# Moving the sum of squares of one norm from TensorE to GpSimd, and two products in pieces between the sums of the next

## The reference

```
mix = token_mixer(a, ...)                      # ends in  concat(h_ml, h_mla) @ w_out
x = x + rmsnorm_2(mix, norm_post_mix)          # "post_mix": mean of mix^2 over the channels
m = rmsnorm_2(x, norm_pre_mlp)                 # "mlp":      mean of x^2 over the channels
y = square(relu(m @ w_up)) @ w_down            # 4096 hidden channels
x = x + rmsnorm_2(y, norm_post_mlp)
```

## Time and profile before

| | |
|---|---|
| median of 3 runs | 2695.09 us (2694.74 to 2695.11) |
| the profiled execution | 2693.12 us |
| its span, first to last instruction | 2691.4 us |
| mean granted TensorE clock | 0.994 |
| PE busy | 2595.1 us (96%) |
| DVE busy | 1857.9 us (69%) |
| ACT busy | 1042.9 us (39%) |
| POOL busy | 1224.1 us (45%) |

### The profile page before, as it was taken

One profiled execution on the slowest core, in us unless ns is written; L12 is line 12 of the kernel. 1 busy time (PEld: TensorE's weight loads), 2 busy tenths in 40 slices (PEclk: granted clock), 3 DMA queues, 4 the chain that ended last, 5 costly groups with the idle time before them and its releaser, 6 DMA issues.

```text
span 2691.4 us, 32407 instructions
## 1 busy us (share of the span) xinstructions
PE 2595.1 (96%) x12366; PEld 2089.7 (78%) x12366; DVE 1857.9 (69%) x2108; ACT 1042.9 (39%) x1447; POOL 1224.1 (45%) x763
## 2 busy tenths in 40 slices
PE   7999999999999999999998999989998999999998
PEld 5888787887777888887886788656885888877777
DVE  7565665457658666668879647766558666778887
ACT  5223343323124333234435111756555433434444
POOL 2222222233447888884333433241135888723331
PEclk9999999999999999999999999999999999999999
DMA  5333333244332433245641343401323554754543
GB/s 192 118 102 114 121 94 126 83 152 155 130 130 63 118 102 111 81 133 199 215 137 55 132 152 101 126 1 46 131 83 84 172 155 147 220 156 160 164 141 141
DMA packets 335840, 339.49 MB, mean 126 GB/s; under 512 B 19723, under 2 KB 254838, under 8 KB 335686
## 3 DMA queue, kind: packets, MB, share of 16 engines
q1 hardware_dynamic: 329446, 313.81, 37.3%
q10 hardware_dynamic: 6240, 23.59, 2.3%
HBM read 228.55 MB, written 107.77 MB: 125 GB/s over the span
## 4 chain that ended last, share of the span: by engine, by line
PE 52%; DVE 10%; issue 2%; ACT 1%; DMA 1%; POOL 1%; SPq 0%; DVEq 0%; ACTq 0%; POOLq 0%
PE ps L3712 36%; PE ps L566 9%; DVE op_lo L3789 2%; PE ps L2784 2%; PE ps L2807 1%; DVE sw_lo L3622 1%; PE ps L2794 1%; DVE acc L4033 1%; DVE acc L4040 1%; PE ps L3288 1%; DVE acc L2310 0%; DVE x L2731 0%; DMA x_block<-acc 0%; DVE op_lo L3692 0%; PE ps L3673 0%
## 5 line engine op out<-in xcount | busy, mean ns | idle before, releaser
L3712 PE MATMUL ps<-op_hi,sw_hi 128*128 128x512 f32 x1769 | 693.2, 392 | 15.8 <-DVE op_lo L3789 8.4
L3712 PE MATMUL ps<-op_hi,sw_lo 128*128 128x512 f32 x1769 | 689.7, 390 | 0.0
L3712 PE MATMUL ps<-op_lo,sw_hi 128*128 128x512 f32 x1769 | 689.5, 390 | 0.0
L3712 PEld LDWEIGHTS ps<-op_hi,sw_hi 128*128 128x128 f32 x1769 | 332.8, 188 | 96.6 <-issue 16.7
L3712 PEld LDWEIGHTS ps<-op_hi,sw_lo 128*128 128x128 f32 x1769 | 332.8, 188 | 69.7
L3712 PEld LDWEIGHTS ps<-op_lo,sw_hi 128*128 128x128 f32 x1769 | 333.0, 188 | 68.9 <-issue 0.5
L532 POOL TENSOR_TENSOR w_hi_t<-w_raw,ones 128x1024 fp32r<-128x1024 f32 (+1 forms) x60 | 118.5, 1978 | 531.1 <-DMA w_raw<-in_w_in 238.0
L3612 ACT ACTIVATE sw_hi<-sw_sumNone 128x512 fp32r<-128x512 f32 (+1 forms) x252 | 157.1, 624 | 332.2 <-PE ps L3712 250.0
L3622 POOL TENSOR_TENSOR sw_lo<-sw_sumNone,sw_hi 128x512 fp32r<-128x512 f32 x138 | 213.8, 1559 | 34.2 <-ACT sw_hi L3612 34.1
L3573 POOL TENSOR_TENSOR sw_sumNone<-sw_raw 128x512 f32<-128x512 f32 (+1 forms) x63 | 113.8, 1806 | 232.1 <-DVE sw_lo L3622 209.3
L3612 ACT ACTIVATE sw_hi<-sw_raw 128x512 fp32r<-128x512 f32 (+1 forms) x189 | 117.5, 622 | 198.1 <-PE ps L3712 196.4
(11 more groups left out here) (500 smaller groups left out, 5423.5 us busy)
## 6 DMA issues: line engine op xcount, KB each, us to landing
op_raw<-hidden SPq DMA_DIRECT2D x42, 1024.0 KB, 8.7
w_raw<-in_w_in SPq DMA_DIRECT2D x47, 512.0 KB, 4.6
sw_raw<-in_w_ffn_in SPq DMA_DIRECT2D x44, 512.0 KB, 5.2
hidden<-hidden_blocks SPq DMA_DIRECT2D x13, 1536.0 KB, 6.1
hidden<-hidden_blocks SPq DMA_DIRECT2D x14, 1280.0 KB, 5.0
sw_raw<-in_w_up SPq DMA_DIRECT2D x32, 512.0 KB, 8.6
sw_raw<-in_w_down SPq DMA_DIRECT2D x32, 512.0 KB, 5.5
acc<-proj SPq DMA_DIRECT2D x30, 512.0 KB, 4.5
```

The costliest lines, as they stand in the source:

```text
L3712: mm = pe.matmul(out, w, x[:, k, :], start=(k == 0 and i == 0 and r < 4), stop=(k == n - 1 and i == 2), skip_group_check=r >= 4)
```

## The change

*First half.* The eight sums over partitions on PE (32 small matmuls) go. The ring of two buffers becomes an accumulator and one buffer: ACT writes the squares of tile 0 to `sq_first0` and those of tiles 1 to 7 to `sq_first1`; POOL adds the second to the first after each tile (`first_squares`, seven instructions). PE sums the accumulator once over the partitions (`first_square_sum`, 4 matmuls), ahead of `half_spread(1)`. ACT's square of tile n (n from 2) now waits for POOL's add of tile n-1. ACT's copy of product M2 (`first_act`) also waits for PE's one sum. POOL's first three adds stand in front of the low part of the last unit's weights, the other four behind it and in front of all that POOL does for the MLP.

*Second half.* The two fp32 products M2+2 and M2+3 are cut in four pieces (`product_block`) of one instruction each, and one piece of each is issued behind every second tile of the loop.

```
             def behind(i):
-                for n in {3: (0, 1), 4: (2, 3, 4), 5: (5, 6, 7)}.get(i, ()):
-                    square_sum3(pe, 0, n)
                 for n in {4: (0, 1), 5: (2, 3)}.get(i, ()):
                     x3_turn(pe, 0, n)
...
             x3_turn(pe, 0, 5)
+            first_square_sum(pe)
             half_spread(pe, 1)
...
+        def first_squares(pool, n):
+            pool.wait_ge(*count("x3_squared", n + 1))
+            if n > 1:
+                pool.wait_ge(*count("x3_summed", n - 1))
+            a, b = sq_ring[0]
+            pool.tensor_tensor(a[:, :], a[:, :], b[:, :], ALU.add).then_inc(count("x3_summed", 0)[0], 1)
+
+        def first_square_sum(pe):
+            pe.wait_ge(S["rstd_ready"], NORM_AT[PM[0]] + 1)
+            pe.wait_ge(*count("x3_summed", KT - 1))
+            for c in range(4):
+                mm = pe.matmul(PS[2][:, c * P:(c + 1) * P], sq_ring[0][0][:, c * P:(c + 1) * P], ones[:, :],
+                               start=(c == 0), stop=True, skip_group_check=True)
+            mm.then_inc(count("x3_summed", 0)[0], 1)
...
-                act.activation(sq_ring[t][n % 2][:, :], acc[:, XO[t][n], HT[t]], ACT.Square)\
+                act.activation(sq_ring[t][n % 2 if t else min(n, 1)][:, :], acc[:, XO[t][n], HT[t]], ACT.Square)\
...
+        def product_block(pe, m, k):
+            p, r = SEQ[m]
+            if k == 0:
+                pe.wait_ge(*count("sw_sum", 4 * p + {1: 2, 6: 4}[r]))
+            if r == 6:
+                pe.wait_ge(*count2("b_hi", KT + k + 1))
+            else:
+                pe.wait_ge(*count2("t_made", 2 * k + 2))
+            mm = pe.matmul(bank(p, r), weight_block(p, r)[:, k * P:(k + 1) * P], fresh_of(p, r)[:, k, :],
+                           start=(k == 0), stop=(k == 3))
+            if k == 3:
+                mm.then_inc(S["s_product"], 1)
...
             act.wait_ge(*count("s_product", done(p, 0)))
...
+            if p == P2:
+                act.wait_ge(*count("x3_summed", KT))
...
             for n in range(KT):
                 square_sum3(pe, 1, n)
                 x3_turn(pe, 1, n)
-            product_fp32(pe, M2 + 2)
+                if n % 2:
+                    product_block(pe, M2 + 2, n // 2)
+                    product_block(pe, M2 + 3, n // 2)
             norm_spread(pe, "mlp")
-            for m in range(M2 + 3, M2 + 7):
+            for m in range(M2 + 4, M2 + 7):
...
-            for n in range(2, len(TILES2)):
+            for n in range(2, len(TILES2) - 1):
                 split_lo(pool, Step(U_WO2 + n))
+            for n in (1, 2, 3):
+                first_squares(pool, n)
+            split_lo(pool, Step(U_END - 1))
+            for n in range(4, KT):
+                first_squares(pool, n)
             x3_pool(pool)
```

## The result

The changed kernel takes 2703.95 us (median of 8 runs, 2702.91 to 2705.9) against 2694.80 before (8 runs): ratio 1.0036, 95% interval 1.0027 to 1.0045. That is 9.2 us slower; 2702.7 had been forecast. The profiled execution took 2705.83 us, its span 2704.1, with a mean granted clock of 0.989.

A forecast was written before the change was run, and what follows sets the result against it. PE, 96% busy, was taken as the bound, with the spread of half 1 and PE's time from loop to M2+6 deciding. Terms 8.8 + 1.6 - 4.3 + 1.5 = +7.6 us gave 2702.7 us (+0.28%), range 2696 to 2708.

The forecast's parts named there:

- Unit 13: Matmul unit awaiting POOL's low part of its weights: starts at 2007.2, 0.2 us earlier, after PE waits 4 us.
- The half's sum of squares complete at 2026.8: DVE's last nine instructions of half 0, slowed by 7 POOL turns of 1.0 us; complete at 2016.05 before.
- The clock, +1.6: Half sums after PE's 13 us idle run at half rate: +1.6 us, bounds 0 and 3.2.
- The spread at 2030.4: Start of half 1's spread on PE, against 2021.56 before: +8.8 us, PE saving included.
- The loop, -4.3: Loop of half 1: pieces fill PE's waits, four rounds take 17.6 to 18.4 us against 22.0 with two products.
- Behind the loop, +1.5: From the loop to M2+6: extra delay from DVE's queue and perhaps the clock, bounds 0 and +3.
- the forecast's first reason: Behind the loop, DVE's own queue holds post_u2; PE's wait before M2+6 grows from 1.88 to about 3.3 us.
- The second reason: Behind the longer wait before M2+6 the clock may be at the lower level again.
- Rival 1: At block_lo DVE goes first, losing 1 to 3 turns, not 7: -1 to +2, 2694 to 2697; chance 0.13.
- Rival 2: POOL's adds find only DVE's gaps, sum of squares by about 2019: 2691, or 2689; chance 0.08.
- Rival 4: The loop's pieces hold up the next round's squares: -1 and not -4.3, 2706; chance 0.04.
- rival 3: POOL contends with DVE through pair P2+1, clock falls twice in full: +11 to +14, 2706 to 2709; chance 0.12.

The follow-up runs named there:

- after: The changed kernel with both halves of the change, against the kernel before it: 2703.95 us, ratio 1.0036.
- second execution of after: The whole change, unaltered, executed and profiled once more: 2703.29 us (one run).
- block sums: Second half of the change alone, plus DVE's last four block sums of half 1 moved ahead of its mean of norm "mlp": 2690.67 us, 0.9987 of before.
- squares only: First half of the change alone, loop and M2+2 as before, against the kernel before: 2706.32 us, ratio 1.0043.
- sum ahead: Whole change, with DVE's last add of the half's squares behind two block_lo, the half's mean behind four: 2696.57 us, 2.2 above before.
- weight sums late: Whole change, with POOL's three weight sums of the first pair moved behind two low parts and DVE's first residual of half 1: 2699.96 us.
- pieces only: Second half of the change alone, the pieces of M2+2 and M2+3 put into the kernel before: 2692.16 us, ratio 0.9989.
- PE kept busy: Whole change, with 46 small matmuls ahead of the half sum to fill PE's idle time: 2701.95 us, 2.0 below the whole change.

## Why the prediction was right, point by point

- *Unit 13* (forecast: waits 4 us, starts 0.2 earlier). It waited 4.53 us and started, corrected, at 2007.90: 0.5 later. Right that the PE time saved in front of it is all waited away. The 0.7 us between the two starts are the 0.77 that ACT's square of tile 3 waited for POOL's second add: I had ACT's split at 2003.4, it was at 2004.1.
- *The half's sum of squares complete at 2026.8.* It was at 2029.90 less 2.42, 2027.5. The seven turns of 1.0 us in DVE's last nine instructions were there: 11.45 + 1.74 against 5.38 + 0.68 is 7.1 us, and three of them measured apart are 3.07. The 0.7 us too much are those of the point above: `block_lo` started at 2014.4 where I had 2013.7.
- *The clock, +1.6.* This term was mis-sized. It rested on one row, 3.2 us of work at half rate behind 6.50 us of idle time. Here it was 5.4 us behind 10.92, and 4.5 us behind the 4.53 before unit 13. Keeping PE busy measured the term at 2.6 us.
- *The spread at 2030.4 and 1.6 more for the clock: 2032.0.* It was 2033.8: 0.7 of the difference is the sum's, 1.1 the clock's.
- *The loop, -4.3.* Measured -4.5 in after, -4.4 alone. Rounds 4.38 us, no wait.
- *Behind the loop, +1.5.* Measured +1.7 up to the late row: M2+4 stands 7.7 us late, the late row 9.4. 1.4 of it is made as the forecast's first reason had it, of PE's waits for DVE (2.22, 0.52, 1.48 and 0.33 us against 1.88, 0.94 and 0.36). The second reason, a second fall of the clock, did not happen in after; where it happened it cost next to nothing at the late row. I had a wait of 3.3 before M2+6, it was 2.22; M2+6 stands at 2072.0, where I had 2071.
- *The sum.* +7.6 was forecast, the late row has +9.4 and the median +9.2. The clock accounts for 1.1 of the 1.8 us, the sum of squares for 0.7, the term behind the loop for 0.2, and the loop gave 0.2 back. To their ends the two profiles of after show +10.3 and +10.2, 1 us of it behind the late row, which no term of the forecast has; that the median lies as near to the late row as it does is in part luck.

Rival 1 (DVE gets through) needed lengths of 0.7 in `block_lo`. Rival 2 needed the sum by 2019. Both are out by the DVE rows. Rival 4 (the loop doesn't give) is out by the rounds of 4.38 us without a wait. Of rival 3 a part came true: the clock was out in the open for longer than I had taken.

One wait remains. Behind the late row PE waits for DVE a second time, 1.33 us in before and 2.35 in after, since DVE's first instruction of a product starts late there. The profile puts DVE's idle time down to `issue`, so to nothing that it knows of. The timeline of DVE in before and in after:

```profile
2364.73 0.69 DVE L3728 TENSOR_TENSOR s_u<-ps,s_p 128x512 f32<-128x512 f32 x1 [0.48 <-issue]
```

```profile
2377.60 0.69 DVE L3760 TENSOR_TENSOR s_u<-ps,s_p 128x512 f32<-128x512 f32 x1 [1.51 <-issue]
```

The instruction reads `s_p`, and that is written by ACT. The timeline of ACT in before and in after:

```profile
2361.73 1.92 ACT L3782 ACTIVATE op_hi<-op_raw 128x2048 fp32r<-128x2048 f32 x1 [2.90 <-DMA op_raw<-hidden]
...
2364.07 0.58 ACT L3721 ACTIVATE s_p<-ps 128x512 f32<-128x512 f32 x1
```

```profile
2374.60 1.91 ACT L3814 ACTIVATE op_hi<-op_raw 128x2048 fp32r<-128x2048 f32 x1 [3.93 <-DMA op_raw<-hidden]
...
2376.94 0.58 ACT L3753 ACTIVATE s_p<-ps 128x512 f32<-128x512 f32 x1
```

ACT's copy ends 0.08 us before DVE starts, here as in all the other profiles to within 0.01 us, and it stands in ACT's queue behind a split that waits for a transfer of `hidden`. Against the late row that split starts 1.03 us later in after (1.64 us ahead of it, 2.67 in before), and DVE's instruction 1.03 us later too. So DVE waits for a transfer, by way of ACT. DVE's idle time was 1.01 us in the second execution of after, 0.17 to 0.51 in the four kernels without the squares on POOL, 0.86 to 1.51 in all with them. Why the transfer lands later with them was not tested.

## What to carry to other kernels

An instruction that is moved to an engine which shares a port with a busy one costs the busy one a whole turn, here 1.0 us, and what counts is how many turns lie in front of the result for which the bottleneck waits: here 6.5 us of work taken off TensorE cost 12 us, and changing two places in DVE's queue gave 7 of them back. Small independent products between two waits are the safe half of such a change; judge each half by itself. And before a wait is removed, look whether the next wait behind it is for the same engine: then much of what is won ends there, and so does what the clock takes: half of what I had expected of the block sums, and nearly all of the 1.7 us of M2+6 at half rate.

## What the runs showed of the hardware

- Two full queues on DVE and POOL alternate one by one, at 1.02 us of DVE per POOL instruction of 128x512 fp32. The pattern held over eight instructions in a row in before (first MLP, DVE's starts 1.70 us apart from 832.87 to 844.76, of which the earlier trace rows has two) and over five in after (from 2020.98).
- The granted clock fell to 0.50 behind waits of TensorE as short as 1.87 us (squares only) and 1.93 us (sum ahead), and stayed at 1.00 behind 1.88 (before), 2.21 (weight sums late) and 2.22 and 2.21 us (after, twice), while it fell behind 2.21, 2.21 and 2.22 us in three others (pieces only, PE kept busy, sum ahead). Of waits of this length one cannot say from their length alone whether the clock falls. In the wait of 10.92 us it fell during the wait (0.67 in the mean of 2021 to 2023 us); behind the 1.87 and 1.93 us only 1.2 us into the work that followed. The Trainium skill (TensorE: Matmul & The Clock Gate, "HAM oscillation — how this bites in real kernels") describes a fall at each longer wait for data in a matmul kernel; these rows show it also at short ones, and not at each.
- The time at half rate behind a fall was 4.5 us of work (unit 13), 5.4 (half sum, after), 3.2 and 3.4 (M2+1, sum ahead), so one row is a poor base for it.
